# The mLSTM value projection of a two-block model as seven block products with token blocks stationary

## The reference, cut to what matters

```python
h = rms_norm_2(x, norm_pre)
proj = h @ w_in
...
qc, kc, vc = to_chunks(q), to_chunks(k) * d ** -0.5, to_chunks(v)
...
sc = jnp.einsum('bhctd,bhcsd->bhcts', qc, kc) * d_intra
num = num + jnp.einsum('bhcts,bhcse->bhcte', sc, vc)
den = den + jnp.sum(sc, axis=-1)
h = num / jnp.maximum(jnp.abs(den), jnp.exp(-m_t))[..., None]
```

## Time and profile before

| | us |
|---|---|
| median of 3 runs | 2170.3 |
| lowest and highest run | 2168.5, 2170.43 |
| the profiled execution, its own time | 2167.41 |
| its span, first to last instruction | 2165.6 |
| PE busy | 1859.7 (86%) |
| DVE busy | 1036.2 (48%) |
| ACT busy | 408.3 (19%) |
| mean granted TensorE clock | 0.944 |

### The profile page before, as it was taken

One profiled execution on the slowest core, in us unless ns is written; L12 is line 12 of the kernel. 1 busy time (PEld: TensorE's weight loads), 2 busy tenths in 40 slices (PEclk: granted clock), 3 DMA queues, 4 the chain that ended last, 5 costly groups with the idle time before them and its releaser, 6 DMA issues. The chain is left out here.

```text
span 2165.6 us, 27491 instructions
## 1 busy us (share of the span) xinstructions
PE 1859.7 (86%) x11570; PEld 1163.1 (54%) x11570; DVE 1036.2 (48%) x1612; ACT 408.3 (19%) x787; POOL 0.2 (0%) x4
## 2 busy tenths in 40 slices
PE   8999976666767778766676999999999999999998
PEld 5687833333223333322232798974447798974445
DVE  7858522111112222221212668778663558778662
ACT  1123300000000000000000233323323233323322
POOL 0000000000000000000000000000000000000000
PEclk9999999988988888998879999999999999999999
DMA  7222899999999999999999443365433443464430
GB/s 315 78 78 103 327 432 430 434 428 432 430 431 431 432 429 432 429 433 429 433 430 410 170 147 127 144 235 204 162 148 117 141 156 122 148 242 189 175 136 20
DMA packets 32375, 595.02 MB, mean 275 GB/s; under 512 B 3966, under 2 KB 5248, under 8 KB 7560
## 3 DMA queue, kind: packets, MB, share of 16 engines
q1 hardware_dynamic: 30344, 584.31, 65.5%
q10 hardware_dynamic: 1920, 9.09, 1.3%
HBM read 590.22 MB, written 1.06 MB: 273 GB/s over the span
## 5 line engine op out<-in xcount | busy, mean ns | idle before, releaser
L2305 PE MATMUL ps<-ring,arena 128*32 128x512 f32 x2032 | 287.1, 717 | 169.6 <-DMA ring<-in_w_experts 160.9
L906 PE MATMUL ps<-ring,arena 128*128 128x512 f32 x656 | 286.4, 592 | 0.0
L2305 PEld LDWEIGHTS ps<-ring,arena 128*32 128x32 f32 x2032 | 72.9, 128 | 367.2 <-issue 233.0
L906 PEld LDWEIGHTS ps<-ring,arena 128*128 128x128 f32 x656 | 124.3, 190 | 155.0 <-issue 155.0
L2339 PE MATMUL ps<-ring,arena 128*32 128x256 f32 x2016 | 149.2, 446 | 51.6 <-DMA ring<-in_w_experts 50.2
L720 PE MATMUL ps<-arena,ring 128*128 128x128 f32 x1536 | 183.0, 275 | 0.9 <-ACT ring L1049 0.9
L720 PEld LDWEIGHTS ps<-arena,ring 128*128 128x128 f32 x1536 | 177.3, 192 | 3.2 <-issue 1.9
L2970 DVE COPY arena<-ps 128x256 f32<-128x256 f32 x64 | 27.2, 425 | 258.1 <-PE ps L2339 258.1
L720 PE MATMUL ps<-early,ring 128*128 128x128 f32 x1152 | 137.1, 275 | 0.0
L720 PEld LDWEIGHTS ps<-early,ring 128*128 128x128 f32 x1152 | 133.3, 192 | 1.2 <-issue 1.0
L2339 PEld LDWEIGHTS ps<-ring,arena 128*32 128x32 f32 x2016 | 70.0, 125 | 117.0 <-issue 71.9
(11 more groups left out here) (478 smaller groups left out, 2473.3 us busy)
## 6 DMA issues: line engine op xcount, KB each, us to landing
ring<-in_w_experts SPq DMA_DIRECT2D x88, 4096.0 KB, 23.4
ring<-in_w_layers SPq DMA_DIRECT2D x64, 2048.0 KB, 7.7
ring<-in_w_experts SPq DMA_DIRECT2D x13, 2048.0 KB, 11.8
ring<-in_w_first SPq DMA_DIRECT2D x9, 2048.0 KB, 8.2
early<-in_w_layers SPq DMA_DIRECT2D x6, 2048.0 KB, 8.3
arena<-in_w_mem SPq DMA_DIRECT2D x4, 2048.0 KB, 20.7
ring<-in_w_first SPq DMA_DIRECT2D x4, 512.0 KB, 5.7
early<-in_w_experts SPq DMA_DIRECT2D x1, 2048.0 KB, 25.6
```

Of the source, the lines that this page charges most:

```text
L906: last = pe.matmul(ps[:, bank, :], lhs[:, k, :], rhs[:, k, :], start=(first and k == 0), stop=(k == n - 1), skip_group_check=True)
L2305: last = pe.matmul(ps[CAP * e:CAP * (e + 1), v // 4, :], xg[:, (v % 4) * 2 + k, CAP * e:CAP * (e + 1)], w[:, k, e, :], start=(v % 4 == 0 a ...
```

## The change

`ml_v` leaves `ON_TOKENS` and becomes a halved piece of its own kind, `VALUES`: seven block products, with the token block stationary (128x128) and two strips of the weight block moving, so that the result still has tokens on its partitions. One product is four matmuls of 128x256. The chain no longer breaks at `ml_v`, so `ml_v` and `ml_z` are woven into their neighbours like the others, VectorE makes the weight sums of `ml_v` and adds three of its products, and ScalarE copies four. The steps grow by five, and the numbers in `run` are changed for that; `centre_values` of `ml_v` moves behind the multiplication of q and k. Banks of the pieces behind `ml_v` change places by parity, and `gm_u` and `gm_z` change places in two waits; `rt_v` stays whole and writes to banks 7 and 6.

```diff
-ON_TOKENS = ("sb_v", "ml_v", "rt_v", "gm_v")
+ON_TOKENS = ("sb_v", "rt_v", "gm_v")
+VALUES = ("ml_v",)
...
-        def quarter(v, p):
+        def quarter(name, p):
+            v = target[name]
+            if name in VALUES:
+                m, at = {1: (0, 0), 2: (0, 0), 3: (0, SEQ), 6: (1, 0), 4: (1, 0), 5: (1, SEQ)}[p]
+                return v[:, m, at:at + SEQ]
...
-                    for s in range(2):
+                    if name in VALUES:
+                        for k in range(4):
+                            last = pe.matmul(ps[:, bank, 0:SEQ], rhs[:, k, :], lhs[:, :, k, :], start=(p in (1, 2, 7) and k == 0), stop=(k == 3), skip_group_check=True)
+                    for s in range(0 if name in VALUES else 2):
...
-                    run(2 if hd + 1 < NH else 1)
+                    run(2 if hd + 1 < NH else 4)
...
-                run(9)
+                run(11)
...
-                w("ml_vc", 2, 2)
                 w("xa_y", NH, NH)
                 for hd in range(NH):
                     run(2)
+                    if hd == 0:
+                        w("ml_vc", 2, 2)
...
-                        whole(pe, l, "gm_z")
+                        whole(pe, l, "gm_u")
...
-                        run(1)
+                        run(4)
                     w("xt_ps", NH, hd + 1)
...
                 gate_exp("ml_o")
-                run(2)
+                run(4)
                 gate_sigmoid("ml_o")
...
                         convolve("ml_k", 0)
                         mg_rows()
+                        run(3)
                         convolve("ml_k", 1)
...
-                centre_values("ml_v", ml_v, ml_sum, "ml_vc")
                 run(3)
                 w("ml_qks", 1, 1)
...
                 run(2)
-
+                centre_values("ml_v", ml_v, ml_sum, "ml_vc")
+                run(2)
                 gate_bound("ml_o")
```

More of the change, by code:

```diff
@@ L103 @@
 ADDS = [s for s in PRODUCTS if s[1] in (2, 5, 4)]
-TOKEN_JOBS = [(n, i) for n in ("gm_v", "sb_v", "ml_v", "rt_v") for i in range(2)]
+TOKEN_JOBS = [(n, i) for n in ("gm_v", "sb_v", "rt_v") for i in range(2)]
 GATES = ("sb_z", "xa_z", "ml_o", "ml_z", "rt_z", "gm_z")
@@ L509, in build_program @@
                   "ml_q": wide[:, 0:4, 3:3 + SEQ], "ml_k": wide[:, 4:8, 3:3 + SEQ], "ml_o": ml_o, "ml_z": y_all[:, 1],
-                  "rt_q": rt_q, "rt_k": rt_k, "rt_z": y_all[:, 3], "gm_u": gm_u, "gm_z": gm_zt}
+                  "rt_q": rt_q, "rt_k": rt_k, "rt_z": y_all[:, 3], "gm_u": gm_u, "gm_z": gm_zt,
+                  "ml_v": ml_v}
         gate_at = {"sb_z": gate_tmp, "xa_z": gate_tmp, "ml_o": ml_o, "ml_z": gate_tmp, "rt_z": ml_o, "gm_z": gm_rows[:, 1:3, :]}
@@ L532, in bank_of @@
         def bank_of(name, m):
-            return 4 + m if name == "gm_v" else m
+            return {"gm_v": 4 + m, "sb_v": m, "rt_v": 7 - m}[name]
         def after_product(eng, l, name, p):
@@ L937, in layers_pe @@
                     else:
-                        whole(pe, l, "gm_u")
+                        whole(pe, l, "gm_z")
                     product(U_BANK[0], y11, ub11, True, "up_prod")
@@ L1046, in halved @@
                     after_product(act, l, name, p)
-                    dst = quarter(target[name], p)
-                    src = ps[:, SUM_BANK[HALVED.index(name) % 2], 0:SEQ].rearrange("p (s t) -> p s t", s=2)
+                    dst = quarter(name, p)
+                    src = ps[:, SUM_BANK[HALVED.index(name) % 2], 0:SEQ]
+                    if name not in VALUES:
+                        src = src.rearrange("p (s t) -> p s t", s=2)
                     ins = act.mul(dst, src, SCALE) if name == "sb_q" else act.copy(dst, src)
@@ L1057, in run @@
                             m = ("t0", "t1").index(p)
-                            take(name, m, (ml_v if name == "ml_v" else rt_v)[:, m, :])
+                            take(name, m, rt_v[:, m, :])
                         else:
@@ L1336, in add_quarter @@
                     after_copy(dve, l, name, {2: 1, 5: 5, 4: 6}[p])
-                    dst = quarter(target[name], p)
-                    src = ps[:, ADD_BANK[HALVED.index(name) % 2], 0:SEQ].rearrange("p (s t) -> p s t", s=2)
+                    dst = quarter(name, p)
+                    src = ps[:, ADD_BANK[HALVED.index(name) % 2], 0:SEQ]
+                    if name not in VALUES:
+                        src = src.rearrange("p (s t) -> p s t", s=2)
                     if name == "sb_q":
@@ L1549, in centre_values @@
                 def centre_values(name, v, sums, done):
+                    if name in VALUES:
+                        whole(dve, l, name)
                     for m in range(2):
-                        evacuated(dve, job(name, m))
+                        if name not in VALUES:
+                            evacuated(dve, job(name, m))
                         heads = v[:, m, :].rearrange("p (h n) -> p h n", h=NH)
```

## The result

| us | before | changed |
|---|---|---|
| median | 2169.82 (12 runs) | 2176.72 (12 runs) |
| lowest and highest | 2166.17, 2170.43 | 2174.11, 2179.82 |
| span of the profiled execution | 2165.6 | 2176.0 |

The ratio is 1.0037, with a 95% interval of 1.0029 to 1.0045: slower, clear of noise. The ratio is worked out over all the runs and not from the two medians; it stands for +8.0 us (6.3 to 9.8), and the means differ by 7.7, where the medians differ by 6.9. In the experiments they shift by a few lines.

What follows compares the result with a forecast made beforehand. TensorE's summed matmuls were taken to bound the layers. Per layer -1.63 + 3.25 + 0.3 + 0.45 = +2.4 us, +4.7 for both, plus 0.95 for one clock fall: 2170.3 + 5.7 = 2176.0 us, range 2170.0 to 2179.5.

Steps and rivals of the forecast that it cites:

- The matmuls: TensorE's ml_v products: 13.84 us removed, seven products of 12.11 us added; work shrinks by 1.6 us per layer.
- VectorE's chain and the wait: Added sums and adds make ml_conv 5.7 us later; ml_v.5's copy queues behind ScalarE's exponential; TensorE waits 3.25 us at ml_v.3.
- One reading of the prediction: Reading of the busy shares: VectorE is idle half of the layers, but not in front of ml_conv.
- The small waits: TensorE waits per layer behind ml_v.3: 0.3 us for ml_v.4's add before rt_q.2, 0.45 us at the first values.
- The clock: Behind the new wait the clock may fall to half, mean 0.76 over 7 us: 1.7 us of work lost.
- +0.95 per layer where it happens: Net cost of one clock fall behind the wait: 1.7 us lost, 0.75 us of small waits saved; counted once.
- by nine in fourteen: Clock below full behind nine of fourteen first-block gaps; so one fall in two layers was taken as likeliest.
- The gaps in the first block: Fourteen TensorE standstills of 3.10 to 3.28 us, used as the sample for the clock behind the new wait.
- that in which both layers fall: Both layers drop to half clock behind the wait: +6.6 us, 2176.9 us; chance 0.26.
- The rival of no wait: ml_v.5's copy is in time at ml_v.3, only the matmuls count: -3.3 us, 2167.0 us; chance 0.1.
- the turning point of 1350.3: Time of ml_conv at which gain and waits are equal, with a first wait of 0.9 us.
- SP's later unit and the swapped banks: SP's rt_k unit, freed 7 us later, still lands in time; bank swaps of gm_u and gm_z cost nothing.

Runs made afterwards that it cites:

- best_gate: Changed kernel with VectorE's ml_z sums after the convolutions, ScalarE's copies before exponential and logarithm, ml_o's gate sigmoid after the first head's weights: 2165.39 us, ratio 0.9985.
- e_sums: Changed kernel with VectorE's first sums of ml_z moved behind the last three convolutions, ml_o.4's add before them: 2169.03 us, ratio 1.0002.
- e_later: Changed kernel with two more VectorE instructions of 128x1024 (2.4 us) in front of the last three convolutions: 2180.82 us, ratio 1.0056.
- e_copy: Changed kernel with ScalarE's copy of ml_v.5 put ahead of its wait for the convolutions and the exponential: 2173.06 us, ratio 1.0016.
- e_load: Kernel before the change with four more VectorE instructions of 128x1024 (4.9 us) per layer where the change puts its weight sums: 2171.79 us, ratio 1.0009.
- e_warm: Changed kernel with 13 idle matmuls of 128x128 (2.9 us) in front of ml_v.3's wait in each layer: 2173.61 us, ratio 1.0024.

## Why the prediction was right, and where it was not

**The matmuls**: right. -1.63 us per layer was worked out, `best_gate` shows -1.64.

**VectorE's chain and the wait**: right in place and size. `ml_conv` was to come 5.7 us later; the exponential starts 18.87 us after `ml_v.1` instead of 13.15, which is 5.72. The wait was to be 3.25 us; it is 3.24 or 3.25 in both profiles of the change and in both layers. `e_sums`, `e_later`, `e_copy` and `e_load` show each link: the wait follows the chain's length and goes when the copy stands elsewhere, and VectorE's work alone makes little of it. One reading of the prediction is wrong, though nothing in its sum hangs on it: VectorE is not idle half of the layers but a third (busy 652 of 964 us); 48% is its share of the whole span.

**The small waits**: 0.3 and 0.45 us were worked out for full clock. `e_warm`, which has full clock, shows 0.40 and 0.36. In the change itself both are covered by the slower TensorE, as was said.

**The clock**: right in mechanism, short in size. The step that fell short is the term "+0.95 per layer where it happens", counted once, "by nine in fourteen". In both profiles both layers fell, and in each profile one of them lost 2.9 to 3.0 us instead of 1.7 (0.59 and 0.57 over 7 us). The stretches give (41.31 + 40.21 - 2 x 36.83) = +7.9 and (40.19 + 41.47 - 2 x 36.83) = +8.0 us, where 5.7 was forecast; the medians, +6.9 and +6.3, lie between, and by the ratio the change is at +8.0. Beside `e_warm`, whose stretches hold everything but the falls, the clock costs 2.9 and 3.1 us in the two profiles (the small waits that it covers are set off, as in the prediction), where 0.95 was put. That the forecast time, 2176.0 us, lies 0.7 from the median is in part luck: the median of before that it starts from, of three runs, was 0.5 us above that of the twelve. The gaps in the first block stand among less dense work, mostly waits for weights and short matmuls, and seem to have been a poor sample for one that has TensorE at full load on both sides; no run tests this, and full load behind the gap alone does not sort them: behind seven of the fourteen TensorE is busy through all 7 us, and three of the seven fell. Of the rivals, that in which both layers fall came nearest: +6.6. The Trainium skill (TensorE: Matmul & The Clock Gate, section HAM oscillation) tells of a kernel that waits in each tile and starts every tile at half clock. The traces agree with it: the clock fell behind all four waits of the change's size in two profiles, and behind both long waits of `e_later` (the stretches hold 1.7 us more than work and waits). How often a single run escapes a fall is open: the runs of the change spread over 5.7 us, those of before over 4.3.

**The rival of no wait** needed 3.25 us less of VectorE's work. `e_sums` with 2.4 less comes out at the time of before: there the exponential starts at 1350.25 us, beside the turning point of 1350.3 that was worked out. **SP's later unit and the swapped banks** cost nothing: no such line is in the list of waits, and from the first stretch's end to the second's beginning it is 448.65 us now and 448.66 before.

## What to carry to other kernels

Where TensorE never waits, a change that saves its work must be priced by what it adds to the queues of the other engines: walk each queue forward from the profile's durations to the next thing TensorE asks of it. Look above all for a short copy that ends up behind a long instruction that is itself waiting; the order alone was worth 11 us here (+6.9 against -4.2 by the medians, and the same by the stretches), three times what the smaller products save. A new gap of TensorE of some 3 us can cost the clock besides: between dense matmuls it did so in six of six cases here, in the first block in nine of fourteen.

## What was not expected of the hardware

Six waits between dense matmuls, in three profiles (two of the change, one of `e_later`), had 3.08 to 3.99 us of idle time, and behind each the clock fell to 1.2 GHz, for 1.7 to 3.0 us of lost work, while waits of 0.7 to 1.4 us left it full. 13 matmuls that compute nothing, put into the wait, kept it at 2.4 GHz and made the kernel 2.7 us faster by the medians (+6.9 to +4.2) and 2.9 by the stretches. And the first product of TensorE behind a wait takes about 0.1 us more: 1.89 us in `e_copy` for one that otherwise takes 1.79. It need not be the wait that costs this. The two products of `ml_v` behind the small matmuls L853, with no wait in front, take 3.56 us (1346.88 to 1350.44) where twice 1.73 is 3.46.
